# The prompt's selective heads in falling instead of rising order of query blocks, inside a stage shared with the sample group's attention

## The reference, cut to what matters

```python
def dsa_prompt(qa, ka, va, qi, ki, wi, bias_a):
    ...
    def block(i):
        q0 = i * Q_BLOCK                      # 128 queries
        qpos = q0 + jnp.arange(Q_BLOCK)
        idx, valid = select_keys(indexer_scores(sl(qi), sl(wi), ki), qpos, s, topk)
        return dsa_core(sl(qa), ka[b_ix, idx], va[b_ix, idx], valid, qpos[None, :, None] - idx, bias_a)
    out = lax.map(block, jnp.arange(s // Q_BLOCK))     # 8 independent blocks
```

## Time and profile before

| what | us |
|---|---|
| median of 3 runs (lowest, highest) | 2544.35 (2530.52, 2544.56) |
| the profiled execution, its time | 2537.31 |
| its span, first to last instruction | 2535.5 |
| PE busy | 2320.4 (92%) |
| DVE busy | 1080.6 (43%) |
| ACT busy | 736.3 (29%) |
| POOL busy | 687.7 (27%) |
| mean granted TensorE clock | 0.972 |

### The profile page before, as it was taken

How to read it: one execution, slowest core, us unless ns; L and a number is a source line. 1 busy time by engine, 2 the same in 40 slices (tenths; PEclk the granted TensorE clock), 3 DMA queues, 4 the chain that set the end, 5 groups by cost and what they waited for, 6 DMA issues and landing times. The chain is left out here.

```text
span 2535.5 us, 32723 instructions
## 1 busy us (share of the span) xinstructions
PE 2320.4 (92%) x12425; PEld 1562.9 (62%) x12445; DVE 1080.6 (43%) x2405; ACT 736.3 (29%) x2025; POOL 687.7 (27%) x731
## 2 busy tenths in 40 slices
PE   7999998876889888888799899989999999999999
PEld 5644444553555555555544345458888888888887
DVE  5479987762355523343313113344433433370001
ACT  3341245653445445444401014211111111100000
POOL 1131121113455455567500010022221222101110
PEclk9999998998999999999999999999999999999999
DMA  4211101005788788877540203101111111122221
GB/s 142 73 63 68 43 1 42 1 1 192 264 319 312 246 313 304 297 222 205 168 151 1 83 24 142 67 36 51 35 51 34 51 35 51 34 78 69 72 65 39
DMA packets 148609, 281.76 MB, mean 111 GB/s; under 512 B 14486, under 2 KB 83782, under 8 KB 148454
## 3 DMA queue, kind: packets, MB, share of 16 engines
q0 software_dynamic: 49408, 176.19, 20.7%
q1 hardware_dynamic: 80758, 90.50, 10.8%
q10 hardware_dynamic: 18288, 12.98, 1.7%
HBM read 261.68 MB, written 17.94 MB: 110 GB/s over the span
## 5 line engine op out<-in xcount | busy, mean ns | idle before, releaser
L629 PE MATMUL PS<-region 128*128 128x512 f32 (+5 forms) x864 | 327.7, 534 | 1.8 <-DMA region<-w_in 1.8
L2659 PE MATMUL PS<-region,ffn_w 128*128 128x264 f32 x1408 | 323.3, 389 | 1.6 <-PEq L2110 1.6
L2659 PEld LDWEIGHTS PS<-region,ffn_w 128*128 128x128 f32 x1408 | 269.8, 192 | 48.1 <-issue 2.0
L629 PEld LDWEIGHTS PS<-region 128*128 128x128 f32 (+1 forms) x864 | 152.9, 181 | 161.0 <-issue 140.7
L1891 ACT COPY region<-PS 128x512 f32<-128x512 f32 x352 | 193.1, 592 | 179.4 <-PE PS L1770 90.1
L2659 PE MATMUL PS<-region,side 128*128 128x264 f32 x1056 | 243.4, 387 | 1.6 <-POOL side L2616 1.6
L2659 PEld LDWEIGHTS PS<-region,side 128*128 128x128 f32 x1056 | 199.2, 190 | 34.7 <-POOL side L2616 1.7
L909 DVE TENSOR_SCALAR_CACHE_REDUCE mask<-score,cand 128x384 bf16<-128x384 f32 (+2 forms) x198 | 180.7, 942 | 4.2
L1770 PE MATMUL PS<-ident_f,region 128*128 128x128 f32 x1024 | 141.7, 281 | 23.6 <-ACT region L1891 21.2
L1640 POOL DMA_INDIRECT region<-cache_b_k,gather_b x128 | 121.2, 947 | 137.7 <-PE PS L1770 115.3
L1640 POOL DMA_INDIRECT region<-cache_b_v,gather_b x128 | 122.4, 956 | 93.7 <-PE PS L1853 59.7
(11 more groups left out here) (430 smaller groups left out, 3833.2 us busy)
## 6 DMA issues: line engine op xcount, KB each, us to landing
ffn_w<-w_gate SPq DMA_DIRECT2D x11, 1024.0 KB, 5.5
ffn_w<-w_up SPq DMA_DIRECT2D x11, 1024.0 KB, 5.5
region<-w_in SPq DMA_DIRECT2D x4, 2048.0 KB, 7.8
ffn_w<-w_down ACTq DMA_DIRECT2D x7, 704.0 KB, 5.6
region<-x_prompt ACTq DMA_DIRECT2D x8, 512.0 KB, 6.8
region<-x_prompt SPq DMA_DIRECT2D x8, 512.0 KB, 10.5
mem_keys<-cache_mem_k SPq DMA_DIRECT2D x8, 512.0 KB, 4.3
mem_values<-cache_mem_v SPq DMA_DIRECT2D x8, 512.0 KB, 8.1
```

The source lines that it names most:

```text
L629: last = nc.tensor.matmul(M.PS[0:n, s % 3, 0:chunks[j].width], XT[:, c, t * P:t * P + n], w[j % 2][:, c, 0:chunks[j].width], start=(c == 0 ...
L2659: last = nc.tensor.matmul(M.PS[:, bank, 0:TW], left[:, c, :], right[:, c, :], start=begin and c == 0, stop=(c == KH - 1), skip_group_check ...
```

## The change

The list of selective steps is built from block 7 down to block 0 instead of up, and `turned_before` counts its copies for this order. Nothing else is edited: steps, costs, the merge and the sample group's stream stay as they are.

```diff
     steps, n = [], 0
-    for i in range(NB):
+    for i in reversed(range(NB)):
         for p in range(A_H // 2):
             steps += [(what, n, i, p) for what in "LETV"]
             n += 1
...
     def turned_before(n):
-        return sum(1 if m // 4 < 4 else 2 for m in range(n))
+        return sum(1 if NB - 1 - m // 4 < 4 else 2 for m in range(n))
```

## The result

The changed kernel is slower: 2577.4 us (median of 4 runs, 2573.2 to 2582.4) against 2539.9 us (4 runs, 2530.5 to 2544.6), a ratio of 1.0151, 95% interval 1.0127 to 1.0174, so 37 to 38 us. The time lies inside the range given, but the forecast was "within 1%" at 0.62, and what came is the price of the second rival (+30 to +39).

The account below looks back on a forecast made before the run. Bounds: a chain of short steps beside the index, transfers (PE with wide pairs) in B units, POOL's gathers in A units. Terms +6 +3 +11 +2 -5 = +17 us on about 2541 gave 2558 us, range 2536 to 2586.

Parts of the forecast that it names:

- rival 2: Units 0 to 7: transposes stop during ACT's long exponentials, PE has no slack; +30 to +39 us, chance 0.29.
- (b): Index: the first pair beside it goes from 1 to 8 blocks, +6 us (ends 0 and +8).
- (c): Unit 0, second pair: the same added PE work while first gathers arrive, +3 us (ends 0 and +5).
- (d): B units 1 to 31: +27 unit-blocks at a slope of 0.42 us, +11, and +2 for the seven widest pairs.
- (e): A units: PE's relief gives nothing back while POOL issues without pause; shorter gathers -2 us, earlier end -3.
- (a): Price of width on PE: eight blocks 7.5 us, one block 2.4; 5.1 us a pair, 0.73 a block.
- PE alone: B unit beside pairs of eight blocks, if PE alone sets its time: 17.4 us, where the slope gives 14.9.
- The two small gains: A units: gathers shortened beside narrow normalising, -2 us; the last pair's shorter V after the last gather, -3 us.
- rival 3: A units: the granted clock falls, +23 us over the sum, +40 in all, 2581 us; chance 0.05.
- The price of +23: A units with PE at 1.2 GHz throughout: 167 us against 144, +23 us over the sum.

Follow-up runs that it names:

- the swap: Changed kernel with its first two pairs (1024 keys) and last two (128 keys) in each other's places: 3 us gained on chip 10.
- the short exponentials: Changed kernel with each selective exponential over 128 columns of a constant instead of all keys: 1.0109 of the kernel before on chip 10.
- less PE work in T and V: Changed kernel with only key blocks 3, 7 and the last transposed and multiplied with values: 16 us gained on chip 10.
- the rising order with late rounds: Kernel before with the 33 counting rounds in units 16 to 32 instead of 0 to 16: 0.9995 of the kernel before on chip 10.

## Why the prediction was wrong, step by step

The sum was +17 and the stage took +36.6. Of the difference 4 us lie in (b) and (c), 10 in (d) and 5 in (e).

**(a) The price of width on PE** was a little low. A wide pair's T and V took 1.97 and 1.97 us in the changed kernel's index (lines 1387 and 1398, at 625.3 and 635.5 us) as well. But the narrow L of 1.51 us was read where the granted clock was 0.61 (646.0 to 647.6 us); at a clock of 1.00 it took 1.06:

```profile
662.98 0.49 PE L1375 MATMUL PS<-KTA,QTA 64*128 64x128 f32 x4
...
664.04 1.94 PE L1790 MATMUL PS<-region,QBB 128*32 128x256 f32 x32
```

So the pair of eight blocks costs PE about 5.6 us more, 0.8 a block, and not 5.1 and 0.73.

**(b), (c) Index and unit 0: +9 forecast, +13.2 measured.** The mechanism was right, and the swap shows that the whole 13.2 are two pairs' width; my upper ends together allowed 13. It is PE's work, and nearly nothing was hidden. Both wide L steps ran partly at the lower clock (0.8 and 0.7 in those microseconds; timeline of the changed kernel, from each L to what follows it):

```profile
592.97 2.77 PE L1375 MATMUL PS<-KTA,QTA 64*128 64x512 f32 x8
...
597.41 1.04 PE L1704 MATMUL PS<-ident_f,region 128*128 128x128 f32 x8
...
652.81 3.56 PE L1375 MATMUL PS<-KTA,QTA 64*128 64x512 f32 x8
...
658.04 1.04 PE L1770 MATMUL PS<-ident_f,region 128*128 128x128 f32 x8
```

They took 4.4 and 5.2 us in place of 1.6 and 1.5, which is 6.6 more; T and V of the two pairs are 6.1 more. Together 12.7 of the 13.2. The experiments agree: the short exponentials left unit 0 at 96.5 us (0.4 less), and less PE work in T and V took 5.2 us from it.

**(d) is the step that failed: +13 forecast for units 1 to 31, +23.1 measured** (425.7 us before, 448.8 after), and with it the choice between the forecast and rival 2. I divided (14.1 - 12.0) by five blocks and called 0.42 us the price of a block in a unit. But the two ends of that slope are not alike. The narrow end sits on the floor of the transfers (12.0 us, DMA at 0.97), where width is not what sets the time. And the merge counts the counting rounds as steps, so a late unit, without them, also gets fewer selective pairs. Line 1424 alone, which ends each pair (in brackets), for pairs of six blocks in both kernels, before and after:

```profile
977.80:1062.60 84.80, 1.06 (x4) 0.96 0.86 298
```

```profile
792.40:872.70 80.30, 1.06 (x4) 0.98 0.80 262
```

The same four pairs stand beside six units in one kernel and beside five units with ten rounds in the other: 14.1 us a unit against 16.1. My slope took the first for what width costs everywhere. From alike ends it is (17.4 - 12.0)/7 = 0.77 us, my own upper end (21 us for 27 unit-blocks, 0.78). The slope failed where the pairs became wide: 0.42 x 56 unit-blocks is +23.5 us for units 1 to 12, and +39.6 came; 0.42 x 29 is -12.2 for units 13 to 31, and -16.5 came. The units beside eight blocks took 17.4 us, past the 16 us that I had named as the point of decision. That this is to the tenth what "PE alone" would give is luck: with PE's work left whole and only the exponentials short they took 16.0.

Its cause is that of rival 2, PE's work and ACT's exponentials together, with the rounds in the same units beside them. Of the 38 us, 11 go with ACT's long exponentials, 16 with PE's work in T and V, and 12 can be had back by moving the rounds out of the same units; these shares overlap, and are no parts of one sum. I read it as one chain in fixed order, PE, ACT, DVE, PE, in which everything counts once the floor of 12 us is passed; DVE's own part of it was not tested.

And the +23 hide a larger exchange: +39.6 in units 1 to 12, -16.2 in 13 to 33. The gain is small because the late units, relieved, meet the transfers' floor: 12.4 us, DMA at 0.94.

**(e) The A units: -5 forecast, 0 measured.** That PE's relief gives nothing back was right, to 0.1 us. The two small gains didn't come. The gathers beside normalising did get shorter (longest 1065 ns against 1382 in the earlier trace rows), but the stretch stayed 160.3 us, as two of its gathers once started 4.9 us apart, at the last B unit's values, where the same two were 3.1 apart before. The Trainium skill (GPSIMD Engine Reference, 8. Key points) says that GpSimd shares its SBUF interfaces with VectorE; the shorter gathers agree with it in kind. And the last pair's V fell from 3.56 us to 0.70, as worked out, but the end is no nearer to the last gather (timeline of the end, and a window over it, for the earlier trace rows):

```profile
1288.16 0.95 POOL L1640 DMA_INDIRECT region<-cache_a_v,gather_a  x1 [0.30 <-issue]
...
1295.04 0.70 PE L1398 MATMUL PS<-region,VA 128*64 128x128 f32 x4
...
1295.83 1.93 PE L1853 MATMUL PS<-region,sa_pt 128*32 128x128 f32 x32
```

```profile
1288.00:1298.00 10.00, 8.12 (x63) 4.78 (x54) 1.69 (x6) 1.72 (x5) 0.95 (x1) 0.51 0.23 69
```

The values' product starts 7.7 us after the last gather's issue, 8.3 before. The granted clock was 0.51 in this window: the product itself took 1.93 us, where it had 1.10, and three groups of PE's work ahead of it (lines 1802, 1816, 1832) took 2.01, 1.91 and 1.11 us, where they had 1.07, 1.09 and 0.66. Those are 3 us, as much as the shorter V gave. So rival 3 came in part: the clock fell to 0.88 in the A units (0.98 before), with PE busy 106 us in place of 121 and 21.3 us of waits for gathered values in place of 2.1. In all six profiles of the falling order on the first kind, edits included, units 34 to 50 had 0.86 to 0.89, in the four of the rising order 0.95 to 0.97. The Trainium skill (TensorE: Matmul & The Clock Gate, HAM oscillation — how this bites in real kernels) says that short compute between waits for DMA brings the clock down again and again; the A units agree, with 0.88. It cost the tail's gain and nothing more, since POOL held the rest. The price of +23 needed PE at 1.2 GHz throughout.

**Chances.** Rival 2 had 0.29 and the right amount, +30 to +39. What I called the measured slope was the argument for the forecast over it, and it was one from unlike stretches.

## What to carry to other kernels

A slope read from two stretches of a trace is the price of one thing only if the rest is the same in both: count what else stands in each (steps of the other stream, pairs a unit), not only the width. When work is moved from a stretch that one engine bounds to another, price the receiving stretch by all that the moved work brings, on every engine in the chain, and take no room for granted because an engine shows some idle time: a PE at 0.84 had no room left, and a PE at 0.86 beside full DMA had little. Look at the granted clock of a row before its time is used as a price. Measure such a balance on more than one chip, as the bound can change between them.

## What the runs showed of the hardware

- One program took 2538 to 2541 us on one chip and 2673 to 2685 us on three others, with the difference in the single stage that gathers with indirect DMAs (683 against 818 us for the rising order with late rounds); the later work took 1268 to 1273 us on all of them. The change is 1.5% slower on the first kind and 0.3% faster on two of the others.
- Indirect gathers issued back to back start every 1.24 to 1.25 us (0.94 to 0.95 median and 0.30 of issue), whether one moves 256 or 512 KB. 128 of them took 160.3 us with PE busy 121 or 106 of 144 us in the stretch; with two more wide pairs beside them they took 176 us, and on the other chips 189 in the changed kernel.
- Less work for PE came with a lower granted clock in some stretches (0.98 to 0.88 in the A units, 1.00 to 0.90 in units 1 to 3) and not in others (1.00 in units 1 to 3 with the same work left out and the exponentials short). Where it fell in units 1 to 3, the gain was gone: 51.7 us after 52.1.
